# Expert routing in a Trainium2 kernel: 64 candidates a head, a rank-by-rank 16-bit decode, and low pieces made by VectorE from half 21 on

## The reference, cut to what matters

```
s1 = einsum('bshd,hnd->bshn', q[..., 0, :], keys[:, 0])      # 8 heads x 128 scores a token
s2 = einsum('bshd,hnd->bshn', q[..., 1, :], keys[:, 1])
v1, i1 = top_k(s1, 16);  v2, i2 = top_k(s2, 16)              # both sorted, best first
cand = (v1[..., :, None] + v2[..., None, :]).reshape(B, S, 8, 256)
sc, j = top_k(cand, 16)
e1 = take_along_axis(i1, j // 16);  e2 = take_along_axis(i2, j % 16)
experts = e1 * 128 + e2;  gates = softmax(sc)
act = gelu(h . u[experts]);  out = sum over experts of gates * act * v[experts]
```

## Time and profile before

| | us |
|---|---|
| median of 3 runs | 3978.19 |
| lowest, highest | 3973.93, 3978.28 |
| profiled execution: span from first to last instruction | 3980.1 |
| TensorE matmul busy | 3754.4 (94%) |
| VectorE busy | 2967.2 (75%) |
| ScalarE busy | 1828.1 (46%) |
| GpSimd busy | 346.3 (9%) |

### The profile page before, as it was taken

One profiled execution on the slowest core, in us unless ns is written; L12 is line 12 of the kernel. 1 busy time (PEld: TensorE's weight loads), 2 busy tenths in 40 slices (PEclk: granted clock), 3 DMA queues, 4 the chain that ended last, 5 costly groups with the idle time before them and its releaser, 6 DMA issues. The chain is left out here.

```text
span 3980.1 us, 72107 instructions
## 1 busy us (share of the span) xinstructions
PE 3754.4 (94%) x29159; PEld 3408.9 (86%) x29159; DVE 2967.2 (75%) x5883; ACT 1828.1 (46%) x3704; POOL 346.3 (9%) x259
## 2 busy tenths in 40 slices
PE   6999899999799779999999999999999999999898
PEld 6997699998699769899999887898999988898798
DVE  7776677776687676987676956589776778688865
ACT  3444445444354444434444456444344444545443
POOL 0000000000000003840000000067200000000000
PEclk9999999999699889999999999899999999999899
DMA  8757376764267424434444453244444444577354
GB/s 321 275 222 287 132 281 220 282 224 171 96 253 271 150 73 159 159 124 167 168 169 169 155 191 143 85 170 143 144 170 168 167 165 166 207 289 281 143 182 147
DMA packets 119661, 745.30 MB, mean 187 GB/s; under 512 B 13857, under 2 KB 14273, under 8 KB 44833
## 3 DMA queue, kind: packets, MB, share of 16 engines
q1 hardware_dynamic: 118082, 737.57, 50.5%
q10 hardware_dynamic: 416, 2.06, 0.1%
q0 software_dynamic: 832, 1.06, 0.1%
HBM read 738.53 MB, written 1.05 MB: 186 GB/s over the span
## 5 line engine op out<-in xcount | busy, mean ns | idle before, releaser
L972 ACT ACTIVATE weights_high<-weight_ring 128x512 fp32r<-128x512 f32 x2248 | 1294.6, 624 | 1208.4 <-PE bank L200 900.2
L980 DVE TENSOR_TENSOR weights_low<-weight_ring,weights_high 128x512 fp32r<-128x512 f32 x2016 | 1298.5, 687 | 604.3 <-ACT weights_high L972 599.3
L200 PE MATMUL bank<-h_high,weights_high 128*128 128x256 f32 x4800 | 1374.2, 286 | 31.8 <-DVE h_low L711 10.4
L200 PE MATMUL bank<-h_low,weights_high 128*128 128x256 f32 x4800 | 1365.3, 284 | 0.0
L200 PE MATMUL bank<-h_high,weights_low 128*128 128x256 f32 x4800 | 1364.6, 284 | 0.0
L200 PEld LDWEIGHTS bank<-h_high,weights_high 128*128 128x128 f32 x4800 | 927.2, 193 | 50.8 <-issue 27.1
L200 PEld LDWEIGHTS bank<-h_low,weights_high 128*128 128x128 f32 x4800 | 927.7, 193 | 9.5 <-issue 0.9
L200 PEld LDWEIGHTS bank<-h_high,weights_low 128*128 128x128 f32 x4800 | 927.4, 193 | 0.0
L200 PE MATMUL acc<-weights_high,hidden_high 128*128 128x512 f32 x1552 | 613.3, 395 | 0.0
L200 PE MATMUL acc<-weights_low,hidden_high 128*128 128x512 f32 x1552 | 606.4, 391 | 0.0
L200 PE MATMUL acc<-weights_high,hidden_low 128*128 128x512 f32 x1552 | 604.3, 389 | 0.0
(11 more groups left out here) (328 smaller groups left out, 3466.8 us busy)
## 6 DMA issues: line engine op xcount, KB each, us to landing
weight_ring<-stream SPq DMA_DIRECT2D x574, 1024.0 KB, 4.8
h_feat<-slots SPq DMA_DIRECT2D x96, 512.0 KB, 5.8
h_tok<-slots SPq DMA_DIRECT2D x94, 512.0 KB, 5.7
work<-slots SPq DMA_DIRECT2D x26, 512.0 KB, 8.4
mod_sums<-biases SPq DMA_DIRECT2D x7, 1536.0 KB
h_feat<-rows SPq DMA_DIRECT2D x8, 512.0 KB, 4.2
work<-rows SPq DMA_DIRECT2D x7, 512.0 KB, 5.7
work<-biases SPq DMA_DIRECT2D x1, 1536.0 KB
```

Source lines behind the costliest of these rows:

```text
L200: ins = self.nc.tensor.matmul(out, lhs, rhs, start=start, stop=stop)
L972: act.activation(k.w_hi[:, b, q * self.QUARTER:(q + 1) * self.QUARTER], self.raw(g, q), ACT.Copy).then_inc(k.highs_ready, 1)
L980: return eng.tensor_tensor(k.w_lo[:, b, w], self.raw(g, q), k.w_hi[:, b, w].bitcast(F32), ALU.subtract)
```

## The change: what it does

1. Candidates: instead of all 16 x 16 sums a head, 64 are formed, in four blocks (`CAND_ROWS`: rank 0 with ranks 0 to 15, ranks 1 to 3 with 0 to 7, ranks 4 to 7 with 0 to 3, ranks 8 to 15 with rank 0). The second `top16` is over 16 rows of 64. A place among the 64 is turned into its two ranks by a few arithmetic operations on 256 numbers.
2. Decode: the grid is laid out rank by pair (16 x 128), so that each operation runs along 128 adjacent bf16 numbers. The ranks are laid out once, in `KeyScores` (`numbers`). The key numbers are widened to such grids by ScalarE in eight operations at halves 15 to 22 (`widen`).
3. Low pieces: GpSimd makes halves up to 19 (`POOL_HALVES`); VectorE makes all others, thirteen of them (20 to 32) between the routing operations, by calls of `low`.
4. Places: the exponential stands at half 23, the turn after half 33, `split_gates` at step 35 of VectorE's loop; the builds of the first quarter are then spread over halves 37 to 59.

```diff
+CANDS = 64
+CAND_ROWS = ((0, 0, 1, 16), (16, 1, 3, 8), (40, 4, 4, 4), (56, 8, 8, 1))
...
+    def numbers(self, dve):
+        dve.tensor_copy(self.ranks, self.k.c("iota")[:, 0:TOP].unsqueeze(2).to_broadcast([P, TOP, PAIRS]))
+    def widen(self, act, i):
...
+        act.wait_ge(k.ranked, number + 1)
...
+        act.activation(wide, idf[:, at].unsqueeze(3).to_broadcast([P, TOP // 2, PEER_HEADS, TOP]),
+                       ACT.Copy).then_inc(k.widened, 1)
...
-        for t in range(TT):
-            cand = self.cand[:, t, :].rearrange("p (h a b) -> p h a b", a=TOP, b=TOP)
-            ins = dve.tensor_tensor(cand, side(self.val, t, 0).unsqueeze(3).to_broadcast(full),
-                                    side(self.val, t, 1).unsqueeze(2).to_broadcast(full), ALU.add)
+        for first, rank, n, m in CAND_ROWS:
+            shape = [P, TT * PEER_HEADS, n, m]
+            ins = dve.tensor_tensor(every[:, :, first:first + n * m].rearrange("p g (a b) -> p g a b", b=m), ...)
...
+        low(dve)
+        dve.tensor_single_scalar(eighth.bitcast(U32), at, 3, ALU.logical_shift_right)
+        self.step(dve, dve.tensor_single_scalar(fourth.bitcast(U32), at, 2, ALU.logical_shift_right))
+        self.step(dve, dve.tensor_scalar(place, at, -48.0, 0.0, ALU.add, ALU.max))
+        self.step(dve, dve.scalar_tensor_tensor(place, fourth.bitcast(U32), -6.0, place, ALU.add, ALU.max))
+        self.step(dve, dve.scalar_tensor_tensor(place, eighth.bitcast(U32), -1.0, place, ALU.add, ALU.max))
+        low(dve)
+        dve.tensor_copy(a, place)
+        dve.tensor_scalar(eighth, place, 8.0, 8.0, ALU.mult, ALU.add)
+        self.step(dve, dve.tensor_scalar(fourth, place, 4.0, 24.0, ALU.mult, ALU.add))
+        dve.scalar_tensor_tensor(eighth, place, 16.0, eighth, ALU.mult, ALU.min)
+        self.step(dve, dve.scalar_tensor_tensor(fourth, place, 48.0, fourth, ALU.add, ALU.min))
+        self.step(dve, dve.tensor_tensor(eighth, eighth, fourth, ALU.min))
+        self.step(dve, dve.tensor_tensor(b, at, eighth, ALU.subtract))
+        low(dve)
...
+                self.step(dve, dve.tensor_tensor(hot, place[:, t].unsqueeze(1).to_broadcast([P, TOP, PAIRS]), self.ranks,
+                                                 ALU.is_equal))
+                if t == 0:
+                    low(dve)
+                dve.wait_ge(k.widened, 8 * self.host.number + 4 * s + 2 * t + 2)
+                self.step(dve, dve.tensor_tensor(hot, hot, self.wide[TT * s + t], ALU.mult))
+                low(dve)
...
+                    self.step(dve, dve.tensor_tensor(dst, src[:, 0:left, :], src[:, left:, :], ALU.add))
...
+                low(dve)
...
-    TURN_AFTER = 39
-    EXP_AT = 32
+    POOL_HALVES = 20
+    WIDEN_AT = 15
+    EXP_AT = 23
+    TURN_AFTER = 33
...
+    def next_low(self, dve):
+        self.low_piece(dve, self.given, 0)
+        self.low_piece(dve, self.given, 1).then_inc(self.k.first_lows, 1)
+        self.given += 1
...
-        self.route.vector(dve)
-        dve.wait_ge(k.turned, self.number + 1)
-        self.split_gates(dve)
+        self.route.vector(dve, self.next_low)
         for g in range(self.n):
...
+            if g == self.given:
+                self.next_low(dve)
+            if g == self.TURN_AFTER + 2:
+                dve.wait_ge(k.turned, self.number + 1)
+                self.split_gates(dve)
```

More of the change, by code:

```diff
@@ L141, in __init__ @@
         self.routed = ctx.enter_context(nc.semaphore("routed"))
+        self.ranked = ctx.enter_context(nc.semaphore("keys_ranked"))
+        self.widened = ctx.enter_context(nc.semaphore("key_numbers_widened"))
         self.turned = ctx.enter_context(nc.semaphore("routes_turned"))
@@ L1646, in vector @@
         k = self.k
+        self.next.route.numbers(dve)
         for i in range(0, len(self.fills), 2):
@@ L1707, in __init__ @@
         nk = 2 * PEER_HEADS * TOP
-        self.val, self.idx, self.idf = room(TT, nk), room(TT, nk), room(TT, nk)
-        self.cand = room(TT, PEER_HEADS * TOP * TOP)
+        self.val, self.idx = room(TT, nk), room(TT, nk)
+        self.cand, self.ranks = room(TT, PEER_HEADS * CANDS), halfwords(room(PAIRS * TOP // 2), TOP, PAIRS)
+        n = PAIRS * TOP // 2
+        flat = scores.rearrange("p t n -> p (t n)")
+        self.wide = [halfwords(flat[:, i * n:(i + 1) * n], TOP, PAIRS) for i in range(2 * TT)]
+        self.idf = halfwords(room(TT * nk // 2), TT, nk)
         self.best, self.at, self.a, self.b = (side[:, i * TT * PAIRS:(i + 1) * TT * PAIRS].rearrange(
@@ L1717, in scalar, with step, vector @@
         act.activation(self.out[:, 2, :], self.best, ACT.Exp).then_inc(k.scalar_for_vector.sem, k.scalar_for_vector.send())
-    def vector(self, dve):
+    def step(self, dve, ins):
+        ins.then_inc(self.k.dve_step, 1)
+        dve.wait_ge(self.k.dve_step, self.k.step("dve"))
+    def vector(self, dve, low):
         k = self.k
@@ L1734, in vector @@
-        ins.then_inc(k.dve_step, 1)
-        dve.wait_ge(k.dve_step, k.step("dve"))
-        rows = [self.cand[:, t, h * 256:(h + 1) * 256] for t in range(TT) for h in range(PEER_HEADS)]
+        dve.tensor_copy(self.idf, idx).then_inc(k.ranked, 1)
+        side = lambda s: self.val.rearrange("p t (h s j) -> p (t h) s j", s=2, j=TOP)[:, :, s, :]
+        every = self.cand.rearrange("p t (h c) -> p (t h) c", c=CANDS)
+        for first, rank, n, m in CAND_ROWS:
+            shape = [P, TT * PEER_HEADS, n, m]
+            ins = dve.tensor_tensor(every[:, :, first:first + n * m].rearrange("p g (a b) -> p g a b", b=m),
+                                    side(0)[:, :, rank:rank + n].unsqueeze(3).to_broadcast(shape),
+                                    side(1)[:, :, 0:m].unsqueeze(2).to_broadcast(shape), ALU.add)
@@ L1737, in vector @@
+        self.step(dve, ins)
+        rows = [self.cand[:, t, h * CANDS:(h + 1) * CANDS] for t in range(TT) for h in range(PEER_HEADS)]
         cut = lambda b: [b[:, t, h * TOP:(h + 1) * TOP] for t in range(TT) for h in range(PEER_HEADS)]
         top16(k, dve, rows, cut(self.best), cut(at))
-        a, b = (self.val.rearrange("p t (s n) -> p s t n", s=2)[:, i].bitcast(U32) for i in range(2))
-        twice = [P, TT, PAIRS, 2]
-        a2, b2 = (halfwords(x.rearrange("p t n -> p (t n)"), TT, PAIRS, 2) for x in (self.a, self.b))
@@ L1752, in vector @@
-        dve.wait_ge(k.dve_step, k.step("dve"))
+        self.step(dve, dve.tensor_copy(self.sum, best[:, :, 0]))
         dve.tensor_tensor(best, best, self.sum.unsqueeze(2).to_broadcast(n), ALU.subtract).then_inc(k.vector_for_scalar.sem, k.vector_for_scalar.send())
[L1755 to L1758, removed]
+        low(dve)
@@ new lines, in vector @@
+        eighth, fourth = (self.val.rearrange("p t (s n) -> p s t n", s=2)[:, i] for i in range(2))
+        dve.tensor_single_scalar(eighth.bitcast(U32), at, 3, ALU.logical_shift_right)
+        self.step(dve, dve.tensor_single_scalar(fourth.bitcast(U32), at, 2, ALU.logical_shift_right))
+        a, b = (halfwords(x.rearrange("p t n -> p (t n)"), TT, PAIRS) for x in (self.a, self.b))
+        place = self.cand[:, :, 0:PAIRS]
+        self.step(dve, dve.tensor_scalar(place, at, -48.0, 0.0, ALU.add, ALU.max))
@@ L1759, in vector @@
+        self.step(dve, dve.scalar_tensor_tensor(fourth, place, 48.0, fourth, ALU.add, ALU.min))
+        self.step(dve, dve.tensor_tensor(eighth, eighth, fourth, ALU.min))
+        self.step(dve, dve.tensor_tensor(b, at, eighth, ALU.subtract))
+        low(dve)
+        hot = halfwords(self.hot, TOP, PAIRS)
         at = [PAIRS * TOP // 2 + PAIRS * TOP // 2 * i // 4 for i in (0, 2, 3)]
-        halves = [halfwords(self.hot[:, a:], PAIRS, n) for a, n in zip(at, (8, 4, 2))]
-        for s, place in ((0, a2), (1, b2)):
+        halves = [halfwords(self.hot[:, i:], n, PAIRS) for i, n in zip(at, (8, 4, 2))]
@@ L1762, in vector @@
+        for s, place in ((0, a), (1, b)):
             for t in range(TT):
[L1763 to L1768, removed]
@@ L1772, in vector @@
                     left //= 2
-                    dve.tensor_tensor(dst, src[:, :, 0:left], src[:, :, left:], ALU.add).then_inc(k.dve_step, 1)
-                    dve.wait_ge(k.dve_step, k.step("dve"))
+                    self.step(dve, dve.tensor_tensor(dst, src[:, 0:left, :], src[:, left:, :], ALU.add))
                     src = dst
-                dve.tensor_tensor(self.out[:, s, t * PAIRS:(t + 1) * PAIRS], src[:, :, 0], src[:, :, 1],
-                                  ALU.add).then_inc(k.dve_step, 1)
-                dve.wait_ge(k.dve_step, k.step("dve"))
+                self.step(dve, dve.tensor_tensor(self.out[:, s, t * PAIRS:(t + 1) * PAIRS], src[:, 0, :], src[:, 1, :],
+                                                 ALU.add))
+                low(dve)
         dve.wait_ge(k.scalar_for_vector.sem, k.scalar_for_vector.take())
         gate = self.out[:, 2, :].rearrange("p (m j) -> p m j", j=TOP)
[L1781 to L1784, removed]
```

(13 more changed lines are left out.)

28 lines of the change are left out of this document (7 added, 21 removed).

## The result

After takes 3935.15 us (median of four executions), before 3978.24 (also of four): a ratio of 0.9883, 95% interval 0.986 to 0.9906. One of the four of after was disturbed (18253.86) and is left out of the ratio; the others took 3932.04, 3933.52 and 3936.79. The forecast was 3939, range 3928 to 3955. The profiled execution's span fell from 3980.1 to 3935.0, by 45.1. (Halves are counted from 0 in this text, so the first low part that VectorE makes is that of half 20; the title counts from 1.)

The account below looks back on a forecast made before the run. TensorE paces the in-phases and loses 48.4 us there to waits. Gains of 19.8 us in the first layer and 19.0 in the second, together 38.8, lower the median 3978.19 to 3939; range 3928 to 3955.

Parts of the forecast that it names:

- fourteen small operations: VectorE's routing: two for the softmax's maximum, twelve for the ranks, 256 numbers each, at 0.42: 5.9 us.
- thirteen low pairs: VectorE's low parts of halves 20 to 32, between routing operations, at 1.29 each: 16.8 us.
- TensorE held, a layer: TensorE waits for VectorE's low parts over halves 20 to 32, mostly at the first three: 4.8 us.
- The chain: VectorE's work from the end of the additions, 1603.9, to the low part of half 32: 53.2 us, ending at 1657.1.
- Source (1): Waits in before's in-phases: VectorE and GpSimd shut each other out, at the big additions and in the decode.
- (3): Third source of waits: builds pressed into halves 43 to 59 fill VectorE, 20.00 of 20, and TensorE waits for them.
- Source (2): Waits in before at the turn: routing ends late, TensorE idles 4.72 us, then runs at half clock.
- What was priced at nothing: `numbers` before the first bank copy, `widen` on ScalarE, the exponential moved to half 23, the builds: zero expected.
- (a): Rival: additions don't wait for GpSimd, small operations are cheap, TensorE is never held; 3930 us, chance 0.17.
- (b): Rival: decode operations in the new layout run at the fp32 price; 3964 us, chance 0.15 with milder forms.
- (c): Rival: short gaps at each half keep TensorE at 1.2 GHz from half 20 to 36; 3997 us, chance 0.05.
- (d): Rival: the first "out" half is held by something else, so nothing is gained; 3978 us, chance 0.03.

Follow-up runs that it names:

- e1_pool_all: After, but GpSimd makes the low parts of all 64 halves and VectorE none: 3973.64 us, ratio to before 0.9987.
- e8_turn39: After, but with the turn after half 39 again and the builds pressed into halves 43 to 59: 3932.22 us, ratio to before 0.9883.
- e4_cands_only: Before with the 64 candidates alone (four additions, rows of 64, ranks by arithmetic): 3967.86 us, ratio to before 0.9976.
- e2_cand256: After, but with all 256 sums a head again and ranks by shift and mask: 3963.86 us, ratio to before 0.9961.

## Why the prediction was right

| step | predicted | measured |
|---|---|---|
| candidate additions | 5.1 | 4.73 |
| second `top16` | 13.6 | 14.05 |
| fourteen small operations | 5.9 | 4.76 |
| decode, four steps | 16.9 | 17.3 |
| thirteen low pairs | 16.8 | 15.7 |
| low pair of half 32 done | 1657.1 | 1655.4 |
| TensorE held, a layer | 4.8 | 3.1 |
| in-phase | about 208 | 205.82 |
| GpSimd busy | about 115 | 115.9 |

**The chain** was right in each term, within 0.5 us but for two. The small operations took 1.1 a layer less than forecast. Six of the fourteen, `tensor_scalar`s and casts, took 0.28 to 0.30 and not 0.42; that is 0.8. A seventh copies only 16 numbers (0.18), where I had counted 256. The seven two-input operations took 0.42 or 0.43. So the rule of the Trainium skill, "VectorE: DVE Perf Modes", section "The perf-mode tier table", holds here for the kinds of operation that it names: 0.8 us a layer, 1.6 in all, where the estimate from it was 2. The low pairs, the other of the two terms, were 0.08 cheaper each, because an operation behind a pair starts 0.07 to 0.08 before the pair's recorded end (1620.80 + 1.28 and 1622.01).

**Where TensorE is held** was right: 1.44 at half 20 (under 2 was said), then level. The 42.3 us of the in-phases stand against the forecast's 38.8: both layers 1.7 better, which is the 1655.4 for 1657.1.

**Source (1), the two engines shutting each other out,** was right and understated. `e1_pool_all` shows that it is the condition of the whole gain, and `e8_turn39` that what I filed under (3), builds pressed together, was the same source.

**Source (2), "the routing ends late", was wrong.** The stand of 4.72 was there with the routing long done (`e4_cands_only`). It went because after makes the low pairs of the two halves behind the turn (34 and 35) ahead of `split_gates`; `e8_turn39` does so for 40 and 41, and has no stand either. The sum didn't suffer, since I took the lost time from the Gelus and removed all causes at once, and since the price of the new turn was worked out from VectorE's order. That two causes named wrongly cost nothing is owed to this way of adding up, and in part to luck: the change took GpSimd out of the builds as well, and moved the low pairs ahead of `split_gates`.

**What was priced at nothing** was nothing. The copy behind `numbers` starts at its end (1555.91) and its distance to the first Gelu is 10.11, against 10.03 in before. `widen` takes 1.04 (0.95 estimated) and ScalarE still idles 0.51 a half. The exponential only shifts a Gelu: half 21 comes 1.6 late and half 22 catches up, also in `e1_pool_all`, where TensorE doesn't wait there.

**The rivals.** (a), the hidden chain, missed by its additions: they did wait for GpSimd, 4.73 instead of 1.25. Without that wait the chain would have ended at about 1651.9 (my estimate, 1655.4 less 3.5), before TensorE asks for half 32 at 1652.25. (b), a layout that doesn't pack, fell: 1.22. (c), the clock, fell: 1.00 throughout, with two gaps. Its price was real, though. In `e2_cand256` a gap of 13.42 was followed by 0.50, and half 20 came 16.0 late. Of the 2.6 beyond the gap about 0.3 come at full clock too (in after half 20 is 1.7 late behind a gap of 1.44); the other 2.3 I put down to the slow clock. The clock swings that the Trainium skill, "TensorE: Matmul & The Clock Gate", section "A second HAM failure mode: psum-queue depth-cycling", tells of follow on idles that come often; after has two gaps a layer, and no window of it shows a swing. One argument against (c) was weaker than it looked: the builds of before, at 1.00 from 1750 to 1770, had been at 0.79 from 1720 to 1725 and 0.87 in the next 5 us, behind a gap of 1.56. That after's gap of 1.44 had no such sequel is measured, but nothing in the prediction assured it. (d) fell with the result.

## What to carry over

When two engines shut each other out, price short operations by the other engine's instruction, not by their own length: in this kernel a 0.29 us operation cost 1.27 when it started beside a GpSimd piece of 1.28. Moving the helper's work onto the busy engine can then be a gain, if the busy engine has nothing long between the pieces; so cut the long part (here the second `top16`) in the same edit, since each alone gave a quarter or less. A later wait for the helper can have the same root: here GpSimd's pair of pieces went from 2.55 to 3.40 beside the decode. And before a stand is put down to a late producer, look whether the producer was idle just before it.

## What the runs showed of the hardware

- The wait comes per VectorE operation that starts while GpSimd works, whatever its size. Alone and beside GpSimd: 128x2048 bf16 1.22 and 2.20, three sums of 1024, 512 and 256 bf16 1.47 and 4.38, 128x128 0.29 and 1.27, `tensor_scalar` on 256 numbers 0.28 and 1.39, a copy of 16 numbers 0.18 and 1.18. GpSimd pays as well, and more beside long operations. Six pieces take 7.7 alone (6 x 1.28), took 8.31 over the four short additions of after, and 11.67 over the two long ones of before; 24 took 40.82 in the decode of `e1_pool_all`, for 30.7 alone. How the two engines come to wait for each other, no run here shows.
- Row searches don't take part. In `e2_cand256` sixteen MAX8 over 256 numbers take 5.33 while GpSimd works and 5.32 when it is done. Nor did the `tensor_reduce` and the reciprocal of the softmax in before, with GpSimd at work: 0.42 and 0.25, in after, without it, 0.41 and 0.25. A row of 64 costs 0.88 through the five passes, near the line (0.847) drawn through 128 and 256 numbers: there is a fixed part of about half a microsecond a row, and fewer candidates save less than in proportion.
- TensorE's granted clock behind a stand, by windows of 5 us: 1.00 after 0.52 and 1.44 (after), 0.66 after 1.97 and 0.50 after 13.42 (`e2_cand256`); before had 0.68 after 2.02 and 0.50 after 4.72. The length of one gap does not settle it. In before a gap of 1.56 in the builds was followed by a slow stretch, and gaps of 1.57 at 1750.49 and 1760.54 were not (1.00). TensorE's timeline of before, and the window around it:

```profile
1722.16 1.40 PE L200 MATMUL bank<-work,h_tok 128*128 128x32 bf16 x48 [1.56 <-DVE work L2013]
```

```profile
1720.00:1725.00 5.00, 3.44 (x61) 3.27 (x60) 5.00 (x8) 1.53 (x3) 1.48 (x2) 0.79 0.42 175
```

  So the gaps of after, 1.44 the longest, cost little more than their own length (halves 20 to 22 lost 2.6 for 1.96 of gaps), the long ones of before cost a slow stretch as well, and how much room after has to the next slow stretch is not known.
